# HGRN heads and decode attention as one phase: eight half-head units, one beside each decode sequence

## What is computed

```python
# decode attention, for each of 8 sequences: 4 heads, two maps each, 2048 cached keys in 16 pages
s_past = einsum("bqhmd,bshmd->bhmqs", q, past_k)
s_new  = where(causal, einsum("bqhmd,bshmd->bhmqs", q, k_new), -1e30)
p = softmax(concat([s_past, s_new]), axis=-1)
a = p[:, :, 0] - lam * p[:, :, 1]
o = einsum(a, concat([past_v, v_new]))

# HGRN2, 4 heads of 128 x 128, prompt in chunks, samples from their own states
f = lb + (1 - lb) * sigmoid(zf); q = silu(zq); k = 1 - f; v = zi
A[t,s] = sum_k q[t] k[s] exp(b[t] - b[s])        # b: running sum of log f, s <= t
o = A v + (q * exp(b)) S
S = exp(b_end) S + (k * exp(b_end - b))^T v
out = rms(o) * silu(zg)
```

## Time and profile before

| what | time |
|---|---|
| median of 3 runs | 1615.56 us (1608.15 to 1619.8) |
| profiled execution | 1605.99 us |
| its span, first to last instruction | 1604.4 us |
| TensorE busy | 1187.0 us, 74% |
| TensorE weight loads | 887.0 us, 55% |
| VectorE busy | 575.7 us, 36% |
| ScalarE busy | 424.3 us, 26% |
| GpSimd busy | 319.5 us, 20% |

### The profile page before, as it was taken

The page is one execution under the profiler, slowest core; times in us unless marked ns, Lnnn a source line. Parts: engine busy times, 40 slices in busy tenths (PEclk is TensorE's granted clock), DMA queues, the critical chain, the costliest instruction groups (busy, mean ns, idle before and its releaser), DMA issues. The chain is left out here.

```text
span 1604.4 us, 24498 instructions
## 1 busy us (share of the span) xinstructions
PE 1187.0 (74%) x9212; PEld 887.0 (55%) x9212; DVE 575.7 (36%) x950; ACT 424.3 (26%) x726; POOL 319.5 (20%) x353
## 2 busy tenths in 40 slices
PE   4799996889898963565406666599956978999982
PEld 3799995778777852454303333377734434444441
DVE  6222011536353538666325555411151211121131
ACT  6101111444545446655202211421200100111111
POOL 4000000000000015455131344321101211122131
PEclk9999998898989885777757777799967999999985
DMA  3420211212121122220295999582203598887557
GB/s 115 106 81 14 66 28 54 68 42 67 41 67 41 54 99 72 84 85 17 75 356 191 378 374 342 172 300 80 98 14 144 165 280 259 267 264 212 151 123 187
DMA packets 146351, 225.95 MB, mean 141 GB/s; under 512 B 15681, under 2 KB 98882, under 8 KB 146178
## 3 DMA queue, kind: packets, MB, share of 16 engines
q1 hardware_dynamic: 123410, 146.27, 27.7%
q0 software_dynamic: 22848, 78.40, 16.8%
HBM read 180.07 MB, written 46.92 MB: 141 GB/s over the span
## 5 line engine op out<-in xcount | busy, mean ns | idle before, releaser
L2096 PE MATMUL ps<-ring,e_xgT 128*128 x400 | 180.5, 605 | 9.8 <-SPq L2023 9.8
L2096 PEld LDWEIGHTS ps<-ring,e_xgT 128*128 128x128 f32 x400 | 75.7, 194 | 97.0 <-issue 96.9
L1447 PE MATMUL ps<-d_KT,d_q 32*32 32x512 f32 x1024 | 54.1, 903 | 96.1 <-DVE d_KT L1570 96.1
L2054 POOL DMA_INDIRECT y_rows<-e_oE,slot_to x32 | 50.4, 1574 | 278.1 <-issue 226.6
L2119 PE MATMUL ps<-ring,e_hT 128*128 x200 | 92.4, 605 | 16.9 <-ACT e_hT L2149 16.9
L630 PE MATMUL ps<-xh,a_wh 128*128 128x384 f32 (+1 forms) x288 | 101.5, 352 | 0.0
L630 PE MATMUL ps<-xl,a_wh 128*128 128x384 f32 (+1 forms) x288 | 97.4, 338 | 0.0
L630 PE MATMUL ps<-xh,a_wl 128*128 128x384 f32 (+1 forms) x288 | 97.1, 337 | 0.0
L1447 PEld LDWEIGHTS ps<-d_KT,d_q 32*32 32x32 f32 x1024 | 22.9, 130 | 122.0 <-issue 76.9
L1570 DVE STREAM_TRANSPOSE d_KT<-d_K 128x2048 f32<-128x2048 f32 x32 | 72.9, 2294 | 47.3 <-DMA d_K<-in_cache_k 47.2
L2144 ACT ACTIVATE e_sg<-ps 128x256 f32<-128x256 f32 x32 | 12.3, 383 | 261.4 <-PE ps L2096 243.6
(11 more groups left out here) (344 smaller groups left out, 2574.5 us busy)
## 6 DMA issues: line engine op xcount, KB each, us to landing
d_V<-in_cache_v POOLq DMA_DIRECT2D x128, 256.0 KB, 7.3
d_K<-in_cache_k SPq DMA_DIRECT2D x128, 256.0 KB, 7.8
ring<-in_w_gate SPq DMA_DIRECT2D x16, 1024.0 KB, 6.8
ring<-in_w_up SPq DMA_DIRECT2D x16, 1024.0 KB, 12.0
ring<-in_w_down SPq DMA_DIRECT2D x16, 1024.0 KB, 13.9
zT<-a_zs POOLq DMA_DIRECT2D x12, 544.0 KB, 3.0
a_w<-in_w_in SPq DMA_DIRECT2D x12, 512.0 KB, 3.8
y_rows<-ring SPq DMA_DIRECT2D x10, 512.0 KB, 2.6
```

Of the source, the lines that this page charges most:

```text
L1447: ins = pe.matmul(m.ps[32 * h:32 * h + 32, q, :], q4[32 * q:32 * q + 32, j, h, b, :], KT[32 * q:32 * q + 32, 4 * h + j, :, :].rearrange("p ...
L2054: pool.indirect_dma_start(m.y_rows, bass.IndirectOffsetOnAxis(ap=m.slot_to[:, i:i + 1], axis=0), oE[:, i % 2, :], None, compute_op=ALU.add ...
L2096: ins = pe.matmul(m.ps[:, 2 + u, :], xgT[:, u, k, :], up_k[:, bass.ds(r * KD + k, 1), :].squeeze(1), start=(k == 0), stop=(k == KD - 1))
```

## The change

One phase takes the place of two. The prompt's columns are cut into halves of 512, so that there are eight units: unit n is half n % 2 of head n // 2, and the second half carries the 64 sample columns too. Unit n is written beside sequence n of the decode, in one hand-made order for each engine. Most buffers of the HGRN half are halved; keys have two group buffers and values three; there is one map `P`. PSUM is shared: one bank for all levels, two that turn, four for scores and for the turned map, one for the rest.

SyncE issues keys, values, queries (sixteen copies for each sequence, of a quarter of the bytes), new values and the first loads. ScalarE issues the later `zf` and `zq`, `v`, the sample blocks and states, and stores the states; GpSimd issues `zg`. Scaled keys, turned keys and the small new map are written by ScalarE and no longer by VectorE. All four groups of the map are turned before the first values. `halves` and `causal` are allocated earlier in the space that prompt attention frees.

```diff
-            m.qbd = middle.enter_context(nc.sbuf_tensor("qbd", [128, HEADS, DB, 32], F32))
+            m.qbd = middle.enter_context(nc.sbuf_tensor("qbd", [128, DB, HEADS, 32], F32))
...
-            hgrn_phase(nc, a, out, m)
-            decode_phase(nc, a, out, m)
+            heads_and_decode_phase(nc, a, out, m)
...
+def heads_and_decode_phase(nc, a, out, m):
+    W = SEQ // 2
+    WS = W + NS
+    UT = W // 128
+    UNITS = 2 * HEADS
+    BLOCK = 32
+    BLOCKED = 5
+    LEV, TURN, S0, NEW = 0, 1, 3, 7
+    KEYS = PAGES * PAGE
+    KR, VR = 2, 3
+    assert UNITS == DB
...
+        K = sb("d_K", [128, KR, PG, 512])
+        V = sb("d_V", [128, VR, PG, 512])
...
+        def load_states(eng, h):
+            for n in range(DB):
+                eng.dma_start(vblk[n * DS:n * DS + DS, n, :], m.zi[h, SEQ + n * DS:SEQ + n * DS + DS, :]).then_inc(vblk_in, 16)
+            eng.dma_start(Ss[:, :, :], a.state_hgrn[0, :, h, :, :].rearrange("b k v -> k b v")).then_inc(s_in, 16)
...
+            load_z(sp, 0, "f", 1)
+            load_z(sp, 0, "q", 0)
+            sp.dma_start(pt[:, :], a.page_table.rearrange("(o b) n -> o (b n)", o=1)).then_inc(pt_in, 16)
+            load_v(sp, 0)
+            sp.wait_ge(pt_in, 16)
...
+            def load_keys(g):
+                pages = page_numbers(g)
+                if g >= KR:
+                    sp.wait_ge(kt_ready, g - KR + 1)
+                for j, page in enumerate(pages):
+                    sp.dma_start(K[:, g % KR, j, :], kc[page, :, :]).then_inc(k_in[g % KR], 16)
+            def load_values(g):
+                pages = page_numbers(g)
+                if g >= VR:
+                    sp.wait_ge(group_done, g - VR + 1)
+                for j, page in enumerate(pages):
+                    sp.dma_start(V[:, g % VR, j, :], vc[page, :, :]).then_inc(dv_in[g % VR], 16)
+            def load_queries(n):
+                if n >= 2:
+                    sp.wait_ge(scored, n - 1)
+                for qq in range(4):
+                    for j in range(4):
+                        sp.dma_start(q4[32 * qq:32 * qq + 32, n % 2, j, :, :], m.qbd[32 * j:32 * j + 32, n, :, :]).then_inc(q4_in[n % 2], 16)
...
+            for g in range(KR):
+                load_keys(g)
+            load_queries(0)
+            load_keys(KR)
+            sp.wait_ge(pool_step, 1)
+            load_states(sp, 0)
+            load_v(sp, 1)
+            load_keys(KR + 1)
+            for g in range(VR):
+                load_values(g)
+            for n in range(DB):
+                load_new_values(n)
+                if n + 1 < DB:
+                    load_queries(n + 1)
+                for g in range(NPG):
+                    gk, gv = (n + 1) * NPG + g, n * NPG + g + VR
+                    if n + 1 < DB:
+                        load_keys(gk)
+                    if gv < DB * NPG:
+                        load_values(gv)
...
+        def _(pool):
...
+            for n in range(UNITS):
+                u, w = n % 2, wide(n)
+                pool.wait_ge(q_ready, n + 1)
+                times_q(n, 0)
+                pool.wait_ge(eb_ready, n + 1)
+                pool.tensor_tensor(qe[:, u, 0:w], qe[:, u, 0:w], q[:, 0:w], ALU.mult).then_inc(qe_ready, 1)
+                pool.wait_ge(sig["g"], n + 1)
+                pool.tensor_tensor(gate_of(n), gate_of(n), z["g"][:, 0:w], ALU.mult).then_inc(g_ready, 1)
+                if n + 1 < UNITS:
+                    pool.wait_ge(g_ready, n + 1)
+                    load_z(pool, n + 1, "g", 2)
+                for lv in range(1, LEVELS):
+                    times_q(n, lv)
...
+        def _(pe):
...
+            def transpose_map(n):
+                pe.wait_ge(map_ready, n + 1)
+                pe.transpose(PT_NEW, P[:, KEYS:KEYS + DS], m.ident[:, :]).then_inc(new_done, 1)
+                for g in range(NPG):
+                    for j in range(PG):
+                        p = (g * PG + j) * 128
+                        ins = pe.transpose(m.ps[:, S0 + g, j * 128:j * 128 + 128], P[:, p:p + 128], m.ident[:, :])
+                    ins.then_inc(pt_done, 1)
...
+            def values(n, g):
+                i = n * NPG + g
+                pe.wait_ge(pt_ready, i + 1)
+                pe.wait_ge(dv_in[i % VR], (i // VR + 1) * PG * 16)
+                if g == 0:
+                    pe.wait_ge(new_read, n + 1)
...
+            for n in range(UNITS):
+                turn_keys(n)
+                low_levels(n)
+                score(n)
+                state_steps(n)
+                middle_levels(n)
+                far_levels(n)
+                if n % 2:
+                    sample_states(n)
+                transpose_map(n)
+                for g in range(NPG):
+                    values(n, g)
+                new_values(n)
+                output(n)
+                pick(n)
+                mean(n)
...
+        def _(act):
...
+            def gates(n):
+                w = wide(n)
+                act.wait_ge(z_in["f"], n * 16 + 16)
+                if n:
+                    act.wait_ge(ket_done, before(n))
+                act.activation(sn[:, 0:w], z["f"][:, 0:w], ACT.Sigmoid, scale=-1.0)
+                act.activation(z["f"][:, 0:w], z["f"][:, 0:w], ACT.Sigmoid).then_inc(sig["f"], 1)
+                act.wait_ge(z_in["q"], n * 16 + 16)
+                if n:
+                    act.wait_ge(level_done, n * 3 - 2)
+                    act.wait_ge(x_ready, n * LEVELS)
+                    act.wait_ge(qe_ready, n)
+                act.activation(q[:, 0:w], z["q"][:, 0:w], ACT.Sigmoid).then_inc(sig["q"], 1)
+                act.wait_ge(z_in["g"], n * 16 + 16)
+                act.activation(gate_of(n), z["g"][:, 0:w], ACT.Sigmoid).then_inc(sig["g"], 1)
...
+            def load_next(n):
+                act.wait_ge(b_ready, n)
+                act.wait_ge(exp_done, (n - 1) * LEVELS + 1)
+                load_z(act, n, "f", 1)
+                act.wait_ge(q_ready, n)
+                load_z(act, n, "q", 0)
...
+            def states_out(n):
+                h = n // 2
+                if n % 2:
+                    act.wait_ge(sn_step, h * DB + DB)
+                    act.dma_start(out.hgrn_prompt[0, 0, h, :, :], S[:, NT, :]).then_inc(stored, 16)
+                    act.dma_start(out.hgrn_sample[0, :, h, :, :].rearrange("b k v -> k b v"), Sn[:, :, :]).then_inc(stored, 16)
+                    if h + 1 < HEADS:
+                        load_states(act, h + 1)
+                if n + 2 < UNITS:
+                    load_v(act, n + 2)
...
+            for n in range(UNITS):
+                more = n + 1 < UNITS
+                turned_keys(n)
+                if more:
+                    gates(n + 1)
+                    logs(n + 1)
+                    decays(n + 1)
+                    if n + 2 < UNITS:
+                        load_next(n + 2)
+                maps(n)
+                if more:
+                    level_exps(n + 1, 1, 2)
+                new_map_out(n)
+                map_out(n, 0)
+                map_out(n, 1)
+                assemble(n)
+                map_out(n, 2)
+                map_out(n, 3)
+                if more:
+                    level_exps(n + 1, 2, LEVELS)
+                squares(n)
+                states_out(n)
+                norm(n)
...
+        def _(dve):
...
+            for lv in range(1, LEVELS):
+                subs(0, lv)
+                if lv > 2:
+                    keys(0, lv - 3)
+            for n in range(UNITS):
+                more = n + 1 < UNITS
+                for i in range(3):
+                    take(n, i)
+                if n:
+                    finish(n - 1)
+                if more:
+                    queries(n + 1)
+                    cumulate(n + 1)
+                    with_keys(n + 1)
+                    subs(n + 1, 1)
+                maximum(n)
+                states(n)
+                for i in range(3, 6):
+                    take(n, i)
+                if more:
+                    keys(n + 1, 0)
+                sums(n)
+                if n % 2:
+                    sample_states(n)
+                if more:
+                    subs(n + 1, 2)
+                    subs(n + 1, 3)
+                    keys(n + 1, 1)
+                    subs(n + 1, 4)
+                    subs(n + 1, 5)
+                    keys(n + 1, 2)
+                    subs(n + 1, 6)
+                collect(n)
+                picked_out(n)
+                if more:
+                    keys(n + 1, 3)
```

More of the change, by code:

```diff
@@ L958, in _, with strips @@
                 for lv in range(1, LEVELS):
[L959 to L961 removed]
+                    times_q(n, lv)
         @block.tensor
         def _(pe):
[L965 to L968 removed]
+            def strips(n, i, left, right, some):
+                c0 = level_cols(i)
+                for t in range(some):
+                    for s in range(4 if t < UT else 2):
@@ new lines, in new_values, with pick @@
+            def new_values(n):
```

(46 more changed lines are left out.)

1027 lines of the change are left out of this document (397 added, 630 removed).

## The result

The change made the kernel slower by about 1%: 1632.88 us median (1627.33 to 1634.55, 4 runs) against 1615.88 us of the kernel before on the same chip; the ratio is 1.0109 with a 95% interval of 1.0084 to 1.0135. The profiled execution took 1627.33 us with a span of 1625.5 us, 21.1 us above the span of before. Forecast were 1604 us and 11 us less than before: the sign is wrong, and the time lies in the range.

A forecast was written before the change was run, and what follows sets the result against it. Run order and SyncE's in-order issue queue were taken to bound the merged stage: start 55 us, seven steps of 48.5, end 26, so 420 for 431, net -11 us: 1604 us against the median, range 1515 to 1650.

The forecast's parts named there:

- A: From map ready through far levels, map transposes and first value group: 5.0 us even; odd units add sample states, 2.0.
- Rival 4: TensorE stays at 1.2 GHz longer, 2 us more a unit: +14 us, 1618, no change; chance 0.12.
- B: SyncE's queue: value group waiting for the unit's first values, next unit's keys behind it: 13.1 us, plus landing 2.6.
- C: VectorE turns key group 2 and subtracts level 6, then ScalarE's exponential 0.6; chain at 24.6 us.
- D: ScalarE's squares, TensorE's mean, norm's Ln and Exp, turned keys: chain at 29.6 us; odd units add ScalarE's DMA issues.
- E: ScalarE's gates and logs of unit n+2, with two table loads: 5.2 us until the scan may start.
- F: VectorE's scan 1.2 us, two key subtractions beside a GpSimd product 3.0, level 1 0.7; chain at 39.7 us.
- G: Maximum 2.8 us and exponentials 2.4 at the end of a unit, covering the scores; chain at 44.9 us.
- The tail: After the last map: last unit's values, output, samples, pick and mean, norms and writes, 26 us, ending at 1010.
- 1: SyncE's queue does not bind, a unit takes 33 to 39 us: 1517 us; chance 0.20 with its halfway case of 1560.
- rival 2: Key group 2 and last landing: groups land in 7.8 us, not 2.6, +5.2 a unit: 1645 us; chance 0.16.
- 3: Cycle as serial, 43 to 45 us on average, all the start gained: 1570 to 1585 us; chance 0.12.

The follow-up runs named there:

- Keys first: Changed kernel with the next unit's key groups 0 to 2 ahead of the value group that waits, in SyncE's queue: 1582.69 us, ratio 0.9799.
- five links moved: Changed kernel with next unit's keys earlier, query copies on GpSimd, ScalarE's loads late, sample states behind map transposes, GpSimd's wide products late: 1537.7 us, ratio 0.9532.

## Why the prediction was wrong

The mechanism was right, down to its places: a queue, a chain, seven steps that give back what the filling brings. Keys first (50 us less), fewer query copies (nothing), and three further links of the chain (8 to 16 us each) bear it out one by one. What failed is the size of the terms. The forecast was a difference of 431 and 420 us, and the 420 was a sum of some thirty terms, nearly all rounded to what an operation costs by itself; the chain came out at 454.

- **The start and the 431**: the first map was ready at 644.0 us, forecast 640.0; key groups 0 and 1 were issued by 602.0 instead of 600.6 and group 3 by 624.9 instead of 622.5. +4.

The places A to G were read for the step behind unit 1 (odd) and the one behind unit 2 (even):

- **A** (odd 7.0 us forecast, 10.7 measured; even 5.0 forecast, 5.8 measured). The step that failed: prices of transposes and sample states from rows at the higher clock. The transposes were 2.3 us by 1.07 for eight and took 3.62; the sample states were 2.0 by 2.11 and took 3.78. TensorE had been idle 8.51 us ahead of A, and the granted clock in A was 0.50 and 0.57; the same four products took 1.98 us at 1.00. That accounts for 3.0 of the 3.7. Rival 4 named this and priced it at 2 us a unit over A, D and scores; A alone is off by 0.8 and 3.7.
- **B** 13.1 and a landing of 2.6, 15.7 forecast: 16.0 in unit 1, 17.0 in unit 2. The 3.7 us a group were 3.44 and the landing 3.5 instead of 2.6, and the two errors cancel in the odd unit. The choice of the smallest landing was wrong, but that of 7.8 would have been worse.
- **C** 3.9 forecast, 3.6 measured. **D** 5.0 for even units, 5.9 measured; 8.8 for odd, 9.2 measured. The thirteen issues were taken at 5.1 us and took 6.7, but the odd D came out 3.3 above the even one where 3.4 was forecast; moving eleven of them (one in an even unit) gave 9.7 us in all.
- **E** 5.2 forecast, 5.7 and 5.9: sigmoids of 0.67 us each behind each other, two table loads of 1.28.
- **F** 4.9 forecast, 6.9 (odd) and 6.1 (even). The other failed step: GpSimd beside VectorE was charged to the key subtractions alone, at 3.0 us (measured 3.4 and 1.9). The two subtractions of the first level stood at 0.7 us, their price alone, and took 2.0 and 2.9: one of 288 columns 1.67 us, two of 256 columns 1.49 and 1.48. Moving GpSimd's products gave 15.8 us in all, 12.3 of them in the seven steps of the two profiled executions, more than the whole net gain that the prediction forecast. One reading of the earlier trace rows was loose: the GpSimd product printed there starts (685.53) behind the first key subtraction (684.36); the one that this subtraction ran beside stands ahead of it in the trace, from 682.12 for 3.37 us.
- **G** 5.2 forecast, 5.1 measured.
- **The tail** 26 forecast, 30.

In sum, seven steps of 344.0 us (with the 4.6 of SyncE's lag) became 369.8: +25.8, and +4 at each end, so 1010 became 1044. A and F carry it: by the two units read they are off by 5.7 in an odd step and 2.0 in an even one, 3 x 5.7 + 4 x 2.0 = 25. B, D and E add another 1.4 to 2.7 a step; C, the hand-overs (an estimate of 1 us that the terms as read already hold) and the last step (44.6) take that back.

**The rivals.** 1 (the queue does not bind) is false for this order, since VectorE waited 143.5 us for keys. It is what the order of the code hid: with five links moved the steps are 39.4 us, near the 33 to 39 that it gave, and the total is 1538. 2 (slower, by landings of 7.8 us) has the right sign and the wrong cause: landings were 3.5. 3 needed cheap issues on ScalarE and SyncE and got neither. 4 named one true cause of several, at +14. The range held the time because rival 2 had stretched it, by a cause that was not there, and that is luck. The chance of 0.23 for slower was too low: most terms stood at the price of an operation by itself, and such terms err upward (A, D, E, F did; only C and the price of a group in B came out lower).

One number of the prediction said as much: a merged unit "must beat 43 us", and its own chain gave 46 and 52. The gain hung on 87 us of starts and ends alone, so 2 us more a step would have used it up, and it was 3.7.

## What to carry to other kernels

When two stages are merged so that each covers the other, write out for each in-order queue which wait stands ahead of which work: a load for the next unit behind a load that waits for the running unit turns two pipelines into one serial chain, and moving eight issues ahead of it was worth more (50 us) than the merge itself cost (17). Price a chain with rows taken in the state in which it will run, after idle time for TensorE and beside its neighbour for VectorE; and where the forecast is a small difference of large sums, count in which direction each unknown can err, and put the chances there. A slower result with 143 us of idle time on one named wait is no reason to drop a change: its order had 93 us left in it.

## What the runs showed of the hardware

- A group of four page loads issued through registers cost SyncE 3.43 to 3.45 us in most cases (some 3.8), 1.88 of them the issue, in the changed kernel, in two of its versions and in the kernel before with values on SyncE.
- An issue on ScalarE holds its next instruction: the norm started 2.9 us after its input was ready, behind the issues, seven small block loads of which took 3.16 us, 0.45 each.
- A subtraction of 256 or 288 columns on VectorE took 0.42 to 0.45 us alone and 1.48 to 1.67 beside a GpSimd product; one of 64 columns 0.21 and 1.42.
- Four products of 512 columns took 3.78 us at a granted clock of 0.50, right after an idle time of TensorE, and 1.98 us at 1.00, when 3.6 us of transposes stood ahead of them.
